# The last quarter of an MLP's second matrix product by seven block products, with its results gathered by adding DMAs

## The chip, the cores and the metric

The kernel runs on one core of one Trainium2 chip. The metric is the device time in microseconds of one execution; three runs of the kernel before took 972.04, 972.15 and 972.39 us, the median is 972.15 us.

## The reference, cut to what matters

The program computes two transformer blocks over 512 tokens of width 1024. The change touches only the very end, the MLP of the second block, and its last line above all:

```python
x = x + gt1 * (mixed @ w_o[l])
h = rmsnorm_2(x, g_norm2[l]) * (1.0 + sc2) + sh2
x = x + gt2 * (jnp.square(jax.nn.relu(h @ w1[l])) @ w2[l])     # w1: 1024 x 4096, w2: 4096 x 1024
```

Everything is float32. The result x is the program's output, 512 x 1024.

## The kernel before, in words

**Exact products from rounded halves.** TensorE reads operands rounded to the type fp32r. Each operand is therefore split in an upper half (`wh`, `ah`, `hh`: a copy to fp32r) and a lower half (`wl`, `al`, `hl`: the value minus the upper half), and a product takes three matmuls (L2109 to L2111, helper `three`): upper by upper, upper by lower, lower by upper. ScalarE (ACT) writes the upper half of each weight (L702), VectorE (DVE) the lower one (L1264), in four pieces of 512 columns per weight unit. A unit is a 128 x 2048 piece of weights, 1 MB, that SP loads into a buffer `raw` (L549). Two buffers each for `wh` and `wl` mean that a unit's halves can be written once the product before the last one is done.

**The MLP in quarters.** The hidden width of 4096 is worked in four quarters of 1024 (`q` = 0 to 3). In a quarter, eight blocks of 128 hidden columns are computed first (`h @ w1`, four weight units, 24 matmuls a block), and ScalarE takes relu and square of each. Then comes the quarter's share of the second product, 512 tokens x 1024 by 1024 x 1024.

**The second product by seven.** In quarters 0 to 2 this share is computed as a 2 x 2 block product in Winograd's form of Strassen's scheme: seven products P1 to P7 of half size (256 tokens, 512 x 512 of weights) where eight are usual, 24 matmuls each (two token blocks `b`, four pieces `k`, three matmuls). It needs sums of blocks of the activations (computed by VectorE in `halves` and split in `s_hi`, `s_lo`) and sums of blocks of the weights. The sums of weights are made while they are loaded: GpSimd (POOL) issues DMAs that add to what SP has put in the buffer (L2088, here "adding loads"). Over the quarters each product is summed up in `sums`, and its combinations give the blocks C11, C12, C21, C22 of the result: C11 = P1 + P2, U2 = P1 + P6, U3 = U2 + P7, C12 = U2 + P5 + P3, C21 = U3 - P4, C22 = U3 + P5.

**The last quarter is computed directly.** For `q` = 3 the share is taken in the usual eight half products: two halves of columns (`ch`) by two halves of the contraction (`kh`), four token blocks, four pieces, three matmuls. Before that, VectorE combines the sums of the first three quarters into the blocks of C (L1899), multiplies them by the gate row `gt` (L1907) and adds them to the residual `x2` (printed as x1b; L1909). As each pair of token block and column half is done on TensorE, VectorE multiplies it by the gate (L1917) and adds it to `x2` (L1920), and ScalarE issues its store to `out` (L1255), eight stores of 256 KB.

**What sets the order.** It is written out by hand: each engine has one instruction stream, and semaphores tie them (`wl` counts lower halves of weights, `w2` and `w1` finished products, `x3` VectorE's work on sums, `acc` ScalarE's copies of products, `w0` to `w3` and `wa0` to `wa3` loads and adding loads by buffer). An engine that waits holds up all that is behind it in its stream.

Of the kernel before, what the change touches and what calls it, by code (L numbers as in the profile page):

```python
# [25 lines left out]
def plan():  # L26
# [103 lines left out]
def program(nc, x, xcols, wall, wf, poolw, params, fng, wada, crow_in, rel, out):  # L130
# [7 lines left out]
    NW = 44 + 3 * 11 + 8  # L138
# [11 lines left out]
    for q_ in range(4):  # L150
        over += [("w1", 8 * q_ + 2 * j + 2) for j in range(4)]
        over += ([("w2", 14 * q_ + 2 * r + 2) for r in range(7)] if q_ < 3 else
                 [("half", 6), ("w2", 46), ("half", 7), ("w2", 50)])
# [9 lines left out]
    with ExitStack() as ctx:  # L163
        def sb(name, shape, dt=F32, where=ctx):
# [126 lines left out]
        s2, junk_2 = (sgt[:, 0:512], sgt[:, 512:1024]), sgt[:, 1024:1536]  # L291
# [4 lines left out]

        sums = {1: (sum_y[:, 0, :], sum_y[:, 1, :]), 7: (sum_y[:, 2, :], sum_y[:, 3, :]),
                6: (sum_y[:, 4, :], sum_y[:, 5, :]), 5: (sum_y[:, 6, :], sum_y[:, 7, :]), 2: (sum_x[:, :], sum_z[:, :])}

        def sems(of, *names):  # L300
# [6 lines left out]
                 "x0", "x1", "x2", "x3", "gf", "g0", "g1", "gt", "x4", "x5", "x6", "x7", "bt0", "bt1", "kd0", "kd1", "vm0", "vm1", "dv0", "dv1", "v2", "out")  # L307

        t = sems("pe_", "half", "ss0", "rb", "zh", "v", "f", "tpc", "za", "qz", "ku", "y", "g", "up", "out", "tp",
# [32 lines left out]
        for w_ in range(NW):  # L342
            q_, r_ = divmod(w_ - W_MLP - 4, 11)
            p_ = PRODUCTS[r_] if 0 <= q_ < 3 and r_ < 7 else 0
# [16 lines left out]
        def hidden_at(n):  # L361

            q, m = divmod(n, 8)
            return s2[n % 2] if q == 3 else s_f[m][:, 0:512] if m < 4 else tmp[:, m % 2, :]
# [2343 lines left out]
```

## Time and profile before

| | us |
|---|---|
| median of three runs | 972.15 |
| profiled execution, its own time | 972.63 |
| its span on the core | 970.8 |
| PE (TensorE matmul) busy | 956.8 (99%) |
| DVE (VectorE) busy | 675.2 (70%) |
| ACT (ScalarE) busy | 547.9 (56%) |
| POOL (GpSimd) busy | 83.6 (9%) |

The profiled execution's own time is 1.8 us above its span; what lies around the span is not in the trace. Times in the trace are microseconds from the span's start. The granted clock of TensorE is 0.999 of full speed over the span, so nothing below turns on it. A matmul's "busy" includes its pipeline: 0.39 us each, although one starts every 0.227 us.

### The profile page before, as it was taken

What the parts mean: (1) busy time and instruction counts of PE and PEld (TensorE: products, weight loads), DVE (VectorE), ACT (ScalarE), POOL (GpSimd) and SP (SyncE); (2) the same over time, 40 slices, a digit from 0 to 9 for tenths busy, and PEclk for the clock granted to TensorE, in tenths of its full rate; (3) what the DMA queues carried; (4) which work ended last, traced back from release to release, by engine and by line L of the source; (5) the groups of instructions that cost most, each with busy time, mean ns of one, the idle gap of its engine ahead of it and who ended that gap; (6) DMA issues with size and microseconds to landing.
All of it is one profiled execution on the core that took longest, in us unless ns stands there. A gap on an engine that the chain in (4) does not pass through costs nothing.

```text
span 970.8 us, 13132 instructions
## 1 busy us (share of the span) xinstructions
PE 956.8 (99%) x4712; PEld 799.6 (82%) x4712; DVE 675.2 (70%) x1237; ACT 547.9 (56%) x1085; POOL 83.6 (9%) x173
## 2 busy tenths in 40 slices
PE   8999999999999999999999999999999999999998
PEld 7878998888888887777788888798888888888886
DVE  6487887878788767667778886756635853774773
ACT  6348776754223357479897664556635544734520
POOL 4001100111121112000000000110000001000000
PEclk9999999999999999999999999999999999999999
DMA  7205222148797644634534224355867568473201
GB/s 297 87 23 188 66 65 100 51 158 349 284 323 282 163 147 154 262 110 121 163 104 129 67 66 172 132 131 130 226 192 193 153 211 191 113 223 124 87 34 54
DMA packets 36674, 148.70 MB, mean 153 GB/s; under 512 B 9193, under 2 KB 9193, under 8 KB 24706
## 3 DMA queue, kind: packets, MB, share of 16 engines
q1 hardware_dynamic: 23970, 101.41, 30.7%
q0 software_dynamic: 9568, 42.48, 16.5%
q10 hardware_dynamic: 3072, 3.98, 1.2%
q8 instruction: 38, 0.62, 0.2%
q14 instruction: 26, 0.21, 0.1%
HBM read 138.32 MB, written 5.27 MB: 148 GB/s over the span
## 4 chain that ended last, share of the span: by engine, by line
PE 86%; DVE 8%; ACT 3%; issue 1%; DMA 1%; POOL 0%; ACTq 0%; DVEq 0%; POOLq 0%
PE psum L2109 25%; PE psum L2111 25%; PE psum L2110 25%; PE psum L2277 3%; PE psum L2256 2%; PE psum L2306 2%; PE psum L2309 1%; DVE wl L1264 1%; DMA raw<-in_wall 1%; ACT two L1009 1%; PE psum L2540 1%; DVE hl L1304 1%; DVE xt L1300 1%; DVE ah L1411 0%; ACT wh L702 0%
## 5 line engine op out<-in xcount | busy, mean ns | idle before, releaser
L2109 PE MATMUL psum<-hh,wh 128*128 128x512 f32 (+1 forms) x720 | 273.6, 380 | 0.7 <-DVE hl L1304 0.6
L2111 PE MATMUL psum<-hh,wl 128*128 128x512 f32 (+1 forms) x720 | 267.4, 371 | 0.0
L2110 PE MATMUL psum<-hl,wh 128*128 128x512 f32 (+1 forms) x720 | 267.2, 371 | 0.0
L1264 DVE TENSOR_TENSOR wl<-raw,wh 128x512 fp32r<-128x512 f32 x328 | 213.9, 684 | 46.2 <-ACT wh L702 45.6
L702 ACT ACTIVATE wh<-raw 128x512 fp32r<-128x512 f32 x328 | 188.6, 620 | 81.3 <-PE psum L2111 64.7
L2109 PEld LDWEIGHTS psum<-hh,wh 128*128 128x128 f32 x720 | 135.3, 188 | 24.2 <-DVE hl L1304 1.4
L2111 PEld LDWEIGHTS psum<-hh,wl 128*128 128x128 f32 x720 | 135.2, 188 | 23.9
L2110 PEld LDWEIGHTS psum<-hl,wh 128*128 128x128 f32 x720 | 135.5, 188 | 21.2 <-issue 1.0
L2109 PE MATMUL psum<-wh,ah 128*128 128x512 f32 x224 | 88.3, 394 | 0.0
L2111 PE MATMUL psum<-wh,al 128*128 128x512 f32 x224 | 87.3, 390 | 0.0
L2110 PE MATMUL psum<-wl,ah 128*128 128x512 f32 x224 | 87.2, 390 | 0.0
L861 ACT ACTIVATE pth<-psum 128x128 fp32r<-128x128 f32 (+4 forms) x104 | 45.9, 442 | 18.0 <-PE psum L2277 17.2
L1181 ACT ACTIVATE two<-psum 128x512 f32<-128x512 f32 x32 | 19.1, 598 | 62.6 <-PE psum L2111 62.6
L2111 PEld LDWEIGHTS psum<-wh,al 128*128 128x128 f32 x224 | 42.1, 188 | 9.0
L2109 PEld LDWEIGHTS psum<-wh,ah 128*128 128x128 f32 x224 | 42.1, 188 | 8.8 <-issue 0.6
L2277 PE MATMUL psum<-ident,p_sb 128*128 128x128 f32 x272 | 46.9, 274 | 2.4 <-DVE ptl L1476 2.3
L1476 DVE TENSOR_TENSOR ptl<-psum,pth 128x128 fp32r<-128x128 f32 (+1 forms) x96 | 46.0, 480 | 4.3 <-ACT pth L861 3.5
L2110 PEld LDWEIGHTS psum<-wl,ah 128*128 128x128 f32 x224 | 42.1, 188 | 7.9
L2277 PEld LDWEIGHTS psum<-ident,p_sb 128*128 128x128 f32 x272 | 33.5, 140 | 13.4 <-issue 5.5
L836 ACT ACTIVATE p_sb<-p_sb,sm 128x528 f32<-128x528 f32 (+3 forms) x64 | 36.1, 564 | 7.7 <-DVE sm L1451 6.8
L842 ACT ACTIVATE p_sb<-p_sb,sm 128x528 f32<-128x528 f32 (+3 forms) x64 | 35.6, 559 | 0.3
L2109 PE MATMUL psum<-wh,hh 128*128 128x512 f32 x76 | 30.9, 407 | 1.5 <-DVE wl L1264 0.9
(336 smaller groups left out, 1631.1 us busy)
## 6 DMA issues: line engine op xcount, KB each, us to landing
raw<-in_wall SPq DMA_DIRECT2D x78, 1024.0 KB, 5.3
raw<-in_wall POOLq DMA_DIRECT2D x15, 1024.0 KB, 7.8
wa<-in_wada POOLq DMA_DIRECT2D x24, 512.0 KB, 5.9
gt<-in_wada POOLq DMA_DIRECT2D x20, 512.0 KB, 6.2
xt<-in_xcols SPq DMA_DIRECT2D x8, 264.0 KB, 8.4
cb<-c_rows SPq DMA_DIRECT2D x8, 264.0 KB, 3.1
x<-in_x SPq DMA_DIRECT2D x4, 512.0 KB, 10.2
x_kept<-x SPq DMA_DIRECT2D x4, 512.0 KB, 2.8
```

The costliest lines, as they stand in the source:

```text
L702: e.activation(home(w)[0][:, 512 * c:512 * c + 512], raw_of(w, c), ACT.Copy).then_inc(a["wh"], 1)
L836: e.activation(block_p(h, i), block_p(h, i), ACT.Exp, bias=nmx, scale=1.0 if h in FG else -1.0, accum_out=su).then_inc(a["exp"], 1)
L842: e.activation(block_p(h, i), block_p(h, i), ACT.Copy, scale=mx).then_inc(a["norm"], 1)
L861: e.activation(ph[0:rows, PT[j]:PT[j] + w_], bank[bk][0:rows, 0:w_], ACT.Copy).then_inc(a["turn"], 1)
L1264: e.tensor_tensor(home(w)[1][:, cs], raw_of(w, c), home(w)[0][:, cs].bitcast(F32), ALU.subtract).then_inc(v["wl"], 1)
L1476: e.tensor_tensor(dst, bank[bk][0:rows, 0:w_], ph[0:rows, o:o + w_].bitcast(F32), ALU.subtract).then_inc(v["turn"], 1)
L2109: e.matmul(out_, lh, rh, start=start, stop=False, skip_group_check=True)
L2110: e.matmul(out_, lh, rl, start=False, stop=False, skip_group_check=True)
L2111: return e.matmul(out_, ll, rh, start=False, stop=stop, skip_group_check=True)
L2256: ins = e.matmul(dst[:, size * j:size * j + size], q[:, 128 * i:128 * i + 128], k[:, size * j:size * j + size], start=k is k_up, stop=k is ...
L2277: ins = e.transpose(bank[bk][:, 128 * (i - i0):128 * (i - i0) + 128], head(h)[0][:, o:o + 128], ident[:, :])
L2306: ins = e.matmul(out_bank(h)[:, 128 * i0:512], lhs, ph[:, PT[j]:PT[j] + w_], start=(j == 3 and h not in SB), stop=j < 0, skip_group_check= ...
```

## The change

The last quarter's share of the second product is computed by seven products as well, in an order of its own (`LAST_ORDER`: P1, P2, P6, P5, P7, P4, P3). P1, P6, P7 and P4 of it follow one another in the same two PSUM banks, so that U2, U3 and the last quarter's C21 arise there by accumulation; ScalarE copies P1, U2 and U3 out on the way (`last_copy`). P3 is accumulated on P5.

The blocks of C of the first three quarters are still combined by VectorE and multiplied by the gate, but no longer added to the residual by VectorE: GpSimd issues adding DMAs from one place of SBUF to another, two of 256 KB for each of six blocks (`to_residual`: c12, c21, c11, c22, and of the last quarter 11 and 22). They share one semaphore, `res`, and each pair waits for the pair before it to land. The adding load for P4's weights (T4) stands ahead of the last five of these pairs in GpSimd's stream. C21 and C12 of the last quarter are added by VectorE (`last_21`, `last_12`).

SP issues four of the eight stores, for C11 after five pairs (`res` 160) and for C22 after all six (`res` 192); ScalarE issues the other four. SP loads one weight unit more, GpSimd five adding loads more.

```diff
-        for ch, kh in ((0, 0), (1, 1), (1, 0), (0, 1)) if q < 3 else ((0, 0), (0, 1), (1, 0), (1, 1)):
+        for ch, kh in ((0, 0), (1, 1), (1, 0), (0, 1)):
...
-PRODUCTS = (1, 2, 7, 6, 5, 3, 4)
+ORDER = (1, 2, 7, 6, 5, 3, 4)
+LAST_ORDER = (1, 2, 6, 5, 7, 4, 3)
 P_BANK = {1: (2, 3), 2: (0, 1), 7: (2, 3), 6: (0, 1), 5: (2, 3), 3: (4, 5), 4: (6, 7)}
+LAST_BANK = {1: (4, 5), 2: (2, 3), 6: (4, 5), 5: (6, 7), 7: (4, 5), 4: (4, 5), 3: (6, 7)}
 GATHERED = (1, 2, 7, 6, 5)
+def order(q):
+    return ORDER if q < 3 else LAST_ORDER
 X3 = [(q, p, b) for q in (1, 2) for p in GATHERED for b in range(2)]
-X3 += [(3, name, b) for name in ("u2", "u3", "c12a", "c22", "c11", "c12", "c21") for b in range(2)]
-X3 += [(3, op, ch, i) for ch in range(2) for i in range(4) for op in ("*c", "+c")]
-X3 += [(3, op, ch, i) for ch in range(2) for i in range(4) for op in ("*", "+")]
+X3 += [(3, name, b) for name in ("u2", "u3", "c12a", "c12", "c22", "c21", "c11", "*c12", "*c21", "*c11", "*c22",
+                                 "p11", "*11", "*u", "-u", "p22", "*22", "*21", "+21") for b in range(2)]
+X3 += [(3, op, b) for b in range(2) for op in ("*12", "+12")]
...
             o_ = W_MLP + 11 * q_ + 4
-            place.update(zip(range(o_, o_ + 11), (a2, a3, a0, a1, a2, a3, a1, a0, a2, a3, a1) if q_ < 3 else places[q_]))
+            place.update(zip(range(o_, o_ + 11), (a2, a3, a0, a1, a2, a3, a1, a0, a2, a3, a1) if q_ < 3 else
+                             (a2, a3, a0, a2, a1, a0, a3)))
...
+        block_at = {"c11": sums[1], "c12": sums[6], "c21": sums[7], "c22": sums[5]}
+        p1_last = sums[2]
+        u2_last, u3_last = (s_f[0][:, 0:512], s_f[1][:, 0:512]), (s_f[2][:, 0:512], s_f[3][:, 0:512])
...
-                load(u + 4 + (1 if q < 3 else 0), a0)
+                load(u + 4 + 1, a0)
                 e.wait_ge(v["wl"], 4 * (o + 1) + 4)
                 load(u + 4 + 1, a1)
                 e.wait_ge(v["wl"], 4 * (o + 2) + 4)
-                load(u + 4 + (0 if q < 3 else 2), a2)
+                load(u + 4, a2)
                 e.wait_ge(v["wl"], 4 * (o + 3) + 4)
                 load(u + 4 + 3, a3)
+                e.wait_ge(v["wl"], 4 * (o + 5) + 4)
+                load(u + 4 + 1, a3)
                 if q < 3:
-                    e.wait_ge(v["wl"], 4 * (o + 5) + 4)
-                    load(u + 4 + 1, a3)
...
+            for ch, i0, count in ((0, 0, 160), (1, 2, 192)):
+                e.wait_ge(d["res"], count)
+                for i in (i0, i0 + 1):
+                    e.dma_start(out[128 * i:128 * i + 128, 512 * ch:512 * ch + 512],
+                                x2[:, i, 512 * ch:512 * ch + 512]).then_inc(d["out"], 16)
...
+            def last_copy(r, b):
+                e.wait_ge(t["w2"], 42 + 2 * r + b + 1)
+                if r == 0:
+                    e.wait_ge(v["x3"], N_X3[3, "c11", b])
+                else:
+                    e.wait_ge(v["sl"], 48)
+                e.activation({0: p1_last, 2: u2_last, 4: u3_last}[r][b], bank[4 + b], ACT.Copy).then_inc(a["acc"], 1)
...
+                    if q == 3 and r % 2:
+                        for b in range(2):
+                            last_copy(r - 1, b)
...
+            for b in range(2):
+                e.wait_ge(v["x3"], N_X3[3, "+21", b])
+                store(2 + b, 0)
+            for b in range(2):
+                e.wait_ge(v["x3"], N_X3[3, "+12", b])
+                store(b, 1)
...
+            def gated(name, b):
+                c, ch = block_at[name][b], int(name[2]) - 1
+                if (name, b) == ("c12", 0):
                     e.wait_ge(d["gt"], 32)
-                e.wait_ge(v["x3"], N_X3[3, {(0, 0): "c11", (0, 1): "c12", (1, 0): "c21", (1, 1): "c22"}[i // 2, ch], b])
+                e.wait_ge(v["x3"], N_X3[3, name, b])
                 e.tensor_tensor(c, c, gt[:, 1, 512 * ch:512 * ch + 512], ALU.mult).then_inc(v["x3"], 1)
...
+            def last_21(op, b):
+                c, o = tmp[:, b, :], x2[:, 2 + b, 0:512]
+                if op == "*21":
+                    e.wait_ge(t["w2"], 42 + 10 + b + 1)
+                    e.tensor_tensor(c, bank[4 + b], gt[:, 1, 0:512], ALU.mult).then_inc(v["x3"], 1)
+                else:
+                    e.wait_ge(v["x3"], N_X3[3, "*21", b])
+                    e.wait_ge(d["res"], 64)
+                    e.tensor_tensor(o, o, c, ALU.add).then_inc(v["x3"], 1)
+            def last_12(b):
+                c, o = u2_last[b], x2[:, b, 512:1024]
+                e.wait_ge(t["w2"], 42 + 12 + b + 1)
+                e.wait_ge(v["x3"], N_X3[3, "-u", b])
+                e.tensor_tensor(c, bank[6 + b], gt[:, 1, 512:1024], ALU.mult).then_inc(v["x3"], 1)
...
+                    if q == 3 and r == 0:
+                        last_step(gated, "c21")
+                    elif q == 3 and r == 1:
+                        last_step(gated, "c11", "c22")
+                    elif q == 3 and r == 2:
+                        last_step(last_11, "p11")
+                    elif q == 3 and r == 3:
+                        last_step(last_11, "*11")
+                    elif q == 3 and r == 4:
+                        last_step(last_u, "*u", "-u")
+                    elif q == 3 and r == 5:
+                        last_step(last_22, "*22")
+            last_step(last_21, "*21", "+21")
+            for b in range(2):
+                last_12(b)
...
+            def to_residual(name):
+                n = TO_RESIDUAL.index(name)
+                if n:
+                    e.wait_ge(d["res"], 32 * n)
+                src = {"*11": p1_last, "*22": u3_last}[name] if n > 3 else block_at[name[1:]]
+                for b in range(2):
+                    i, ch = 2 * (int(name[-2]) - 1) + b, int(name[-1]) - 1
+                    e.wait_ge(v["x3"], N_X3[3, name, b])
+                    e.dma_start(x2[:, i, 512 * ch:512 * ch + 512], src[b], accum_op=ALU.add).then_inc(d["res"], 16)
...
+                if q < 3:
+                    e.wait_ge(d[f"w{place[o3]}"], 16 * n_load[o3])
+                    add(q, 2, place[o3])
+                e.wait_ge(d[f"w{place[o2]}"], 16 * n_load[o2])
+                add(q, 2, place[o2])
+                e.wait_ge(d[f"wa{place[o2]}"], 192 + 16 * n_add[o2] - 16)
+                add(q, 0, place[o2])
+                if q == 3:
+                    e.wait_ge(d[f"w{place[o3]}"], 16 * n_load[o3])
+                    add(q, 2, place[o3])
+                    to_residual("*c12")
                 e.wait_ge(v["wl"], 4 * o + 4)
                 add(q, 2, a2)
-                e.wait_ge(v["wl"], 4 * (o + 3) + 4)
-                add(q, 3, a1)
+                e.wait_ge(v["wl"], 4 * o2 + 4)
+                add(q, 3, place[o2])
                 if q == 0:
                     gate(1)
+            to_residual("*c21")
+            to_residual("*c11")
+            to_residual("*c22")
+            to_residual("*11")
+            to_residual("*22")
...
+            def last_product(r):
+                p, w = LAST_ORDER[r], W_MLP + 37 + r
+                upper, lower = home(w)
+                for b in range(2):
+                    if p == 1:
+                        e.wait_ge(v["x3"], N_X3[3, "c12", b])
+                    elif p == 2:
+                        e.wait_ge(a["r"], 30)
+                    elif p == 5:
+                        e.wait_ge(v["x3"], N_X3[3, "c21", b])
+                    elif p == 3:
+                        e.wait_ge(v["x3"], N_X3[3, "p22", b])
+                    else:
+                        e.wait_ge(a["acc"], 10 + {6: 0, 7: 2, 4: 4}[p] + b + 1)
+                    for k in range(4):
+                        if b == 0:
+                            e.wait_ge(v["wl"], 4 * w + k + 1)
+                            e.wait_ge(v["sl"], n_sl(3, k if p in (1, 7) else 4 + k, p in (5, 6, 3)))
+                        o = slice(512 * k, 512 * k + 512)
+                        ins = three(bank[LAST_BANK[p][b]], *factor(p, k, b), upper[:, o], lower[:, o],
+                                    k == 0 and p in (1, 2, 5), k == 3)
                     ins.then_inc(t["w2"], 1)
...
-            for m in range(4):
-                w, ch, kh = W_MLP + 37 + m, m // 2, m % 2
-                for i in range(4):
-                    if m == 0:
-                        e.wait_ge(v["x3"], N_X3[3, "c12" if i < 2 else "c21", i % 2])
-                    for k in range(4):
-                        if i == 0:
-                            e.wait_ge(v["wl"], 4 * w + k + 1)
-                            if ch == 0:
-                                e.wait_ge(v["sl"], 36 + 4 * kh + k + 1)
-                        ins = by_rows(w, k, 4 * kh + k, bank[i + (0 if ch else 4)], (ah, al), 128 * i, 128,
-                                      kh == 0 and k == 0, kh == 1 and k == 3)
-                    if kh:
-                        ins.then_inc(t["w2"], 1)
-                if kh == 0:
-                    ins.then_inc(t["half"], 1)
...
+                    product(q, r) if q < 3 else last_product(r)
```

The helpers `last_11`, `last_u` and `last_22` follow the same pattern as `last_21`: `p11` adds P2 from PSUM to the copy of P1, `*11` multiplies by the gate, `*u` and `-u` multiply U2's copy and subtract it from `x2`, `p22` takes U3's copy and P5 from PSUM together, `*22` multiplies by the gate; each is one VectorE instruction for each of two token blocks.

GpSimd's stream from the third quarter's last adding loads on. Before, it ends there:

```order
L2088 DMA raw3<-in_wall 128x2048 [waits dma_w3]
L2088 DMA raw<-in_wall 128x2048 [waits dma_w2]
L2088 DMA raw<-in_wall 128x2048 [waits dma_wa2]
L2088 DMA raw<-in_wall 128x2048 [waits dve_wl] x2
L163 UNCONDITIONAL_BRANCH
```

In the changed kernel, from the fourth quarter's weights on (`raw` and `raw3` are weight buffers, x1b is the residual, the sources are gated blocks of C):

```order
L2172 DMA raw3<-in_wall 128x2048 [waits dma_wa3]
L2172 DMA raw<-in_wall 128x2048 [waits dma_w0]
L2185 DMA x1b<-sum_y 128x512 [waits dve_x3] x2
L2172 DMA raw<-in_wall 128x2048 [waits dve_wl]
L2172 DMA raw3<-in_wall 128x2048 [waits dve_wl]
L2185 DMA x1b<-sum_y 128x512 [waits dve_x3,dma_res]
L2185 DMA x1b<-sum_y 128x512 [waits dve_x3]
L2185 DMA x1b<-sum_y 128x512 [waits dve_x3,dma_res]
```

Five adding loads and twelve adding DMAs into the residual are new; the last ten of the twelve stand behind the adding load for P4, which waits for VectorE's lower half of P6's weights.

VectorE's stream over its last rows before, the fourth column half of the direct product:

```order
L1264 TENSOR_TENSOR wl<-raw,wh 128x512 x4
L1917 TENSOR_TENSOR tmp<-psum,gt 128x512
L1920 TENSOR_TENSOR x1b<-x1b,tmp 128x512
L1917 TENSOR_TENSOR tmp<-psum,gt 128x512
L1920 TENSOR_TENSOR x1b<-x1b,tmp 128x512
```

And in the changed kernel, from P7's weights on (wl is P7's, then P4's, then P3's lower half; sum_x, sum_z the copy of P1, sgt that of U2, gt and s_y that of U3):

```order
L1296 TENSOR_TENSOR wl<-raw,wh 128x512 x4
L1953 TENSOR_TENSOR sum_x<-sum_x,gt 128x512
L1953 TENSOR_TENSOR sum_z<-sum_z,gt 128x512
L1296 TENSOR_TENSOR wl<-raw,wh 128x512 x4
L1960 TENSOR_TENSOR sgt<-sgt,gt 128x512 x2
L1964 TENSOR_TENSOR x1b<-x1b,sgt 128x512 x2
L1971 TENSOR_TENSOR gt<-psum,gt 128x512
L1971 TENSOR_TENSOR s_y<-psum,s_y 128x512
L1296 TENSOR_TENSOR wl<-raw,wh 128x512 x4
L1974 TENSOR_TENSOR gt<-gt 128x512
L1974 TENSOR_TENSOR s_y<-s_y,gt 128x512
```

The work on results now stands between the lower halves of the weights in every product, and the last block that goes by DMA (L1974, `*22`) is ready only after P3's weights. The last two pairs of instructions on VectorE (L1991, L1993) are of the same kind as before. SP's stream ends, in the changed kernel, with the stores:

```order
L565 DMA raw<-in_wall 128x2048 [waits dve_wl] x31
L707 DMA out<-x1b 128x512 [waits dma_res]
L707 DMA out<-x1b 128x512
L707 DMA out<-x1b 128x512 [waits dma_res]
L707 DMA out<-x1b 128x512
L172 UNCONDITIONAL_BRANCH
```

Before, nothing follows the loads on SP.

## Rows read from the trace of the kernel before

**Rows 1.** Page: busy time by engine, and the chain that ended last.

```profile
PE 956.8 (99%) x4712; PEld 799.6 (82%) x4712; DVE 675.2 (70%) x1237; ACT 547.9 (56%) x1085; POOL 83.6 (9%) x173
...
PE 86%; DVE 8%; ACT 3%; issue 1%; DMA 1%; POOL 0%; ACTq 0%; DVEq 0%; POOLq 0%
```

**Rows 2.** Stretches: us, busy (x) PE, PEld, DVE, ACT, POOL; PEclk, DMA share, GB/s.

```profile
920.00:940.00 20.00, 20.00 (x90) 16.57 (x89) 14.72 (x24) 6.10 (x11) 0.00 (x0) 1.00 0.04 14
940.00:960.00 20.00, 20.00 (x90) 16.57 (x89) 8.78 (x14) 2.83 (x5) 0.00 (x0) 1.00 0.11 40
960.00:971.00 11.00, 6.84 (x31) 5.32 (x29) 4.28 (x7) 0.00 (x0) 0.00 (x0) 0.92 0.25 95
```

**Rows 3.** Timeline of VectorE, the end: start, busy, line, tiles, [idle <-releaser].

```profile
958.72 0.69 DVE L1917 TENSOR_TENSOR tmp<-psum,gt 128x512 f32<-128x512 f32 x1 [8.55 <-PE psum L2111]
...
964.16 0.69 DVE L1917 TENSOR_TENSOR tmp<-psum,gt 128x512 f32<-128x512 f32 x1 [1.30 <-PE psum L2111]
...
966.88 0.69 DVE L1917 TENSOR_TENSOR tmp<-psum,gt 128x512 f32<-128x512 f32 x1 [1.30 <-PE psum L2111]
967.60 0.69 DVE L1920 TENSOR_TENSOR x1b<-x1b,tmp 128x512 f32<-128x512 f32 x1
```

**Rows 4.** One line's instructions: ScalarE's stores (L1255).

```profile
L1255 ACTq DMA_DIRECT2D out<-x1b x8: 338/339/357, 938.4 to 968.3; - x8
...
DMA to landing us min/median/max: 2.0/2.1/2.6
```

**Rows 5.** Timeline of ScalarE: the last relu of the third and fourth quarter.

```profile
841.66 0.60 ACT L1181 ACTIVATE two<-psum 128x512 f32<-128x512 f32 x1 [1.41 <-PE psum L2111]
...
845.08 4.26 ACT L702 ACTIVATE wh<-raw 128x512 fp32r<-128x512 f32 x8
...
923.36 0.60 ACT L1181 ACTIVATE two<-psum 128x512 f32<-128x512 f32 x1 [2.99 <-PE psum L2111]
```

**Rows 6.** Timeline of VectorE in the third quarter's products.

```profile
842.95 0.43 DVE L1858 TENSOR_TENSOR s_y<-tmp,s_y 128x256 f32<-128x256 f32 x1 [1.02 <-ACT tmp L1197]
...
846.09 2.49 DVE L1264 TENSOR_TENSOR wl<-raw,wh 128x512 fp32r<-128x512 f32 x4
...
853.30 2.50 DVE L1264 TENSOR_TENSOR wl<-raw,wh 128x512 fp32r<-128x512 f32 x4
```

**Rows 7.** Timeline of GpSimd: its adding loads in the third quarter.

```profile
800.85 0.88 POOL L2088 DMA_DIRECT2D raw<-in_wall  x1 [25.52 <-DMA raw<-in_wall]
812.99 0.87 POOL L2088 DMA_DIRECT2D raw<-in_wall  x1 [11.27 <-DMA raw<-in_wall]
821.12 0.86 POOL L2088 DMA_DIRECT2D raw<-in_wall  x1 [7.25 <-DMA raw<-in_wall]
842.29 0.86 POOL L2088 DMA_DIRECT2D raw<-in_wall  x1 [20.31 <-DVE wl L1264]
856.17 0.88 POOL L2088 DMA_DIRECT2D raw<-in_wall  x1 [13.03 <-DVE wl L1264]
```

**Rows 8.** GpSimd's adding loads (L2088), from 780 us on: issue to landing.

```profile
L2088 POOL DMA_DIRECT2D raw<-in_wall x5: 859/869/877, 800.9 to 856.2; - x5
...
DMA to landing us min/median/max: 7.7/7.9/8.0
```

**Rows 9.** DMA by queue, 842 to 851 us, one adding load: packets, MB, share.

```profile
q0 software_dynamic: 144, 1.05, 61.6%
```

**Rows 10.** DMA by queue, 958 to 971 us, the last four stores.

```profile
q10 hardware_dynamic: 576, 1.05, 21.4%
```

**Rows 11.** GpSimd's plain load of 512 KB (L2041) issued at 400.5 us.

```profile
L2041 POOL DMA_DIRECT2D wa<-in_wada x1: 528/528/528, 400.5 to 400.5; - x1
...
DMA to landing us min/median/max: 3.7/3.7/3.7
```

**Rows 12.** Timeline of VectorE: combining eight blocks of sums in the fourth quarter.

```profile
893.29 4.89 DVE L1899 TENSOR_TENSOR sum_y<-sum_y 128x512 f32<-128x512 f32 x8
```

More of the change, by code:

```diff
@@ L151, in program @@
         over += [("w1", 8 * q_ + 2 * j + 2) for j in range(4)]
-        over += ([("w2", 14 * q_ + 2 * r + 2) for r in range(7)] if q_ < 3 else
-                 [("half", 6), ("w2", 46), ("half", 7), ("w2", 50)])
+        over += [("w2", 14 * q_ + 2 * r + 2) for r in range(7)]
     assert len(over) == NW
@@ L343, in program @@
             q_, r_ = divmod(w_ - W_MLP - 4, 11)
-            p_ = PRODUCTS[r_] if 0 <= q_ < 3 and r_ < 7 else 0
+            p_ = order(q_)[r_] if q_ >= 0 and r_ < 7 else 0
             loaded_[place[w_]] += p_ not in (4, 5)
@@ L1192, in square @@
                 dst, src = hidden_at(n), two[:, n % 2, :]
[L1193 removed]
+                if m < 4:
                     dst = s_f[m].rearrange("p (a b) -> p a b", a=3)[:, 0::2, :]
@@ L1200, in hidden_upper @@
                 q, m = divmod(n, 8)
-                if q < 3 and (m < 4 or part):
+                if m < 4 or part:
                     e.wait_ge(v["s"], 16 * q + (m + 1 if m < 4 else 3 * m - 5))
@@ L1873, in hidden @@
             def hidden(n):
-                if n < 24:
-                    halves(n)
+                halves(n)
                 hidden_lower(n)
-                if n < 24 and n % 8 > 3:
+                if n % 8 > 3:
                     hidden_lower(n, 1)
             def gather(q, p, b):
-                e.wait_ge(t["w2"], 14 * q + 2 * PRODUCTS.index(p) + b + 1)
+                e.wait_ge(t["w2"], 14 * q + 2 * ORDER.index(p) + b + 1)
                 if q == 1:
@@ L1922, in _, with last_step @@
+            def last_step(f, *ops):
+                for op in ops:
+                    for b in range(2):
+                        f(op, b)
             for q in range(4):
@@ L1933, in _ @@
                     if q == 3 and j < 2:
-                        for name in (("u2", "u3", "c12a", "c22"), ("c11", "c12", "c21"))[j]:
-                            for b in range(2):
-                                blocks(name, b)
+                        last_step(blocks, *(("u2", "u3", "c12a", "c12"), ("c22", "c21", "c11"))[j])
                     elif q == 3 and j == 2:
-                        for i in range(4):
-                            add_block(0, i)
-                if q == 3:
-                    break
-                for r, p in enumerate(PRODUCTS):
+                        last_step(gated, "c12")
+                for r in range(7):
                     w = W_MLP + 11 * q + 4 + r
-                    if q and r and PRODUCTS[r - 1] in sums:
+                    if q in (1, 2) and r and ORDER[r - 1] in sums:
                         for b in range(2):
-                            gather(q, PRODUCTS[r - 1], b)
-                    for c in range(4):
-                        lower(w + 1, c)
-            for m in range(4):
-                for s_ in range(8):
-                    slot(W_MLP + 37 + m, s_)
-                    if m % 2 and s_ % 2:
-                        add_last(m // 2, s_ // 2)
-                    if m == 0 and s_ % 2:
-                        add_block(1, s_ // 2)
+                            gather(q, ORDER[r - 1], b)
+                    if q == 3 and r == 5:
+                        last_step(last_22, "p22")
+                    if w + 1 < NW:
+                        for c in range(4):
+                            lower(w + 1, c)
+                    if q == 3 and r == 0:
[13 more added lines that the diff above has]
+                last_12(b)
         @block.gpsimd
```

125 lines of the change are left out of this document (64 added, 61 removed).

## The prediction

> **What bounds the kernel now.** I read the page first: TensorE is busy 99% of the span and makes 86% of the chain that ended last [rows 1]. Then the stretches of the last 50 us: 20.00 us of 20 busy twice, at full granted clock, and in the last eleven 6.84 us, while the DMA engines carry 4 to 25% [rows 2]. So TensorE's stream of matmuls sets the end, and behind its last one a short tail. Its pace comes from VectorE's last rows: a new block of twelve matmuls is taken over every 2.72 us (964.16, 966.88) [rows 3], so a matmul costs 2.72/12 = 0.2267 us. The tail: the last block is multiplied at 966.88, added at 967.60 (to 968.29), its store issued, and the span ends at 970.8 [rows 3]: 3.9 us after the last matmul, 2.5 us of it after the addition; a store lands 2.0 to 2.6 us after issue [rows 4].
>
> **Matmuls.** The direct share is 2 column halves x 2 halves of the contraction x 4 token blocks x 4 pieces x 3 = 192 matmuls, the share by products 7 x 24 = 168. 24 fewer at 0.2267 us are 5.44 us. If nothing else became late, TensorE would end at 961.4 instead of 966.9, the last addition at 962.85, and the span at 965.4.
>
> **Can the weights and sums keep up?** The third quarter is the model, since it does the same by seven. A quarter is (8 + 7) x 24 matmuls = 81.6 us, and the last relu of the two quarters begins at 841.66 and 923.36, 81.7 apart [rows 5]. There ScalarE writes P2's upper halves from 845.08 and VectorE its lower halves from 846.09 [rows 5, 6]; P2 starts at 841.5 + 5.44 = 846.9, and TensorE was not held. Carried over by 81.6: products start at 923.2 (P1), 928.6 (P2), 934.1 (P6), 939.5 (P5), 945.0 (P7), 950.4 (P4) and 955.8 (P3). Ahead of them VectorE has the extra work of `halves` again (pieces of 0.43 us [rows 6]) and the same 14 combinations as now, at 0.61 us each (eight in 4.89 [rows 12]), while of the eight gate multiplications and additions in this stage two multiplications stay. Laid out row by row at these lengths, each weight piece is ready about 1 us or more ahead of its use, except P2's first, with about 0.4 us, as in the third quarter. In the products' stage VectorE has 16 us for six further weight units (2.50 each [rows 6], 15 us) and 26 instructions on results at 0.6 to 0.7 us, 17 us: 32 of 38 us. It is kept busy but in each product the weights come first or after at most four such instructions. P6's unit is the one I need below: ScalarE ends P2's at 928.9, copies P1 out twice (0.6 each), VectorE does the two multiplications of c21 to 931.3, then P6's lower half from 931.3 to 933.8, before P6 starts at 934.1 for its first piece by 2 us. P4's end leaves VectorE with `p22`, 1.3 us, and P3's weights, done by 954.4, ahead of 955.8. Cost 0, with 1 us as my upper bound.
>
> **Adding loads.** Five more of 1 MB. They land 7.7 to 8.0 us after issue [rows 8]. P5's is released by P1's lower half, at about 923.7 (842.29 in the third quarter, and 81.6 on) and lands by 931.9; ScalarE can use it from 934.1. P4's is issued about 0.4 us after P6's lower half (853.30 + 2.50, issued at 856.17 [rows 6, 7]), so at 934.2, and lands at 941.9; it is wanted at 945.0. Both cost 0, with 2 to 3 us of cover.
>
> **The chain of adding DMAs.** This is where I expect the end to be set. Behind P4's adding load in the same stream and queue come five pairs of 256 KB, and each pair waits for the landing of the one before. What a link costs, from rows: an adding load keeps its queue busy 61.6% of 9 us on 16 engines, so 5.54 us each for 1 MB [rows 9], or 1.39 us for 256 KB at the same rate, about twice the plain rate (four stores: 21.4% of 13 us, 0.70 us each [rows 10]), as it has two sources to read. Issue and completion are the rest, 7.7 - 5.54 = 2.16 us. GpSimd needs 0.43 us from a landing to the next issue (821.12 - 812.99 - 7.7 [rows 7]). For a pair: 2.16 + 2 x 1.39 + 0.43 = 5.37 us. I take 5.1, since the issue of a smaller DMA is shorter (0.53 for 512 KB against 0.86 [rows 8, 11]). Bounds: 2.9 us (a plain 256 KB store lands in 2.1 [rows 4], a second 0.34 later, and the wake-up 0.43), and 13.6 us, if each packet of 2 KB took as long as one of 8 KB (2.16 + 2 x 5.54 + 0.43).
>
> Sum: c21's pair waits in the queue behind P4's load, 941.9 + 2 x 1.39 = 944.7. Then c11, c22, 11 and 22, four links of 5.1: 965.1. The last pair's data is ready at 955.6 (behind P3's weights) and does not matter. c12's pair is early, issued about 919. SP wakes (0.3), issues C22's two stores 0.34 apart, the last at 965.7, and 2.4 us later the span ends: 968.1, where TensorE's own path ends at 965.4. Of 5.44 us, 2.7 are given back.
>
> The Trainium skill, "DMA: Bandwidth & Descriptors", section "Anatomy of one DMA — SWDGE (gpsimd) path", gives for a DMA from GpSimd about 2.0 us plus bytes over 436e3 per us. For 1 MB that is an estimate of 4.4 us; the trace disagrees for DMAs that add, with 7.7 [rows 8], while its fixed part agrees with the 2.16 left over above. By that rule a pair would cost about 3.6 us with the wake-up, and the chain would be covered: this is the first rival's time.
>
> Against the medians: the profiled execution took 972.63 us, 1.8 above its span, and the median is 0.5 lower. I take 2.7 from the median: 969.4.
>
> **Rivals.**
> - *The chain is covered* (25%). The end by the chain is 944.7 + 4 x link + 3.0; it equals TensorE's 965.4 at a link of 4.4 us. For it: source and target both lie in SBUF, the nearest row (7.7) has an HBM source; and the fixed part may be less for a small DMA. Against: twice 1.39 us of transfer are already 2.8. Time: 972.15 - 5.4 = 966.7.
> - *The chain costs more than the products save* (12%): slower than before. It decides at a link above 5.8 us (944.7 + 4 x 5.8 + 3.0 = 970.9), and would be measured as slower from 6.3. The mechanism: an adding packet of 2 KB is dearer per byte than one of 8 KB, because reading both operands, adding and writing has a cost of its own for each packet. For it: nothing in the trace has ever added rows under 8 KB. Against: plain packets of 2 KB move at the rate of larger ones, 256 KB in 0.70 us. At half the 8 KB packet's time for each 2 KB packet, a pair costs 2.16 + 5.54 + 0.43 = 8.1, c21 lands at 947.4, and the median would be 972.15 + (947.4 + 32.4 + 3.0 - 970.8) = 984.2. At 6.5 it would be 975.
> - *TensorE is held* (8%): P5's load or VectorE's heavier stream is late. For it: P2's first piece has only 0.4 us. Against: the third quarter shows the same margin without a stall, and every other wait has 1 us or more. A stall of up to 2.7 us hides behind the chain, except one ahead of P6's weights, which moves P4's load and the whole chain with it: with 1.5 us there, 970.9.
> - *The change does not save matmuls' time* (3%), as accumulating four products in one pair of banks made each wait for ScalarE's copies. P4 follows P7 directly: its first block needs the copy of P7's first, 2.7 us after that was done, and a copy takes 0.6. Covered; if not, up to 3 us, and 969 to 970.
>
> **How the numbers follow.** Forecast, the chain set the end with a link between 4.4 and 5.8 us: 52%, 969.4, its own range 967 to 971.9. About 0.2% (1.9 us) is what a measurement of this kernel can tell from no change, so faster means under 970.2, a link under 5.3. I give two thirds of the forecast case to that side: 0.35; with 0.25 for the covered chain and about 0.05 of the small cases it is 0.65. Same: the rest of the forecast (0.17) and parts of the others (0.06), 0.23. Slower 0.12. The range reaches from the covered chain, 966.5, to a link of 5.9 us, 972.5; outside lie most of the slower rival and a little below.
>
> **What would show it.** In the profile after: 168 matmuls behind the last relu at one per 0.227 us, and VectorE's last multiplication at 961.4 instead of 966.88; GpSimd's rows of L2185 from 934.9 on in pairs, 5.1 us from pair to pair, the last at about 960.5; SP's last store (L707) 3 us after ScalarE's last (L1259, 962.9), and the chain of waits that ended last going through SP and GpSimd's DMAs, no longer through VectorE and TensorE. I am wrong if the pairs follow in under 4.4 us or over 5.8, if P4's adding load is not issued near 934.2, or if TensorE shows idle time among the last seven products.

## The result, and the profile after

| | before | after |
|---|---|---|
| median, us | 972.27 (4 runs) | 977.29 (4 runs, 976.98 to 977.68) |
| ratio to before | 1 | 1.0053, 95% interval 1.0041 to 1.0065 |
| profiled execution: span, us | 970.8 | 975.5 |

The kernel became 5.0 us slower, 0.5%, where 2.7 us faster were forecast. The page of the changed kernel, busy time by engine and the chain that ended last which answer to [rows 1]:

```profile
PE 950.7 (97%) x4688; PEld 795.4 (82%) x4688; DVE 688.7 (71%) x1265; ACT 560.6 (57%) x1107; POOL 98.3 (10%) x190
...
PE 79%; DVE 9%; issue 4%; ACT 4%; DMA 3%; POOL 1%; POOLq 0%; ACTq 0%; DVEq 0%
```

TensorE is busy 6.1 us less, 5.4 of them for 24 matmuls fewer (the other 0.7 I did not follow), but its share of the span has fallen from 99% to 97%, and "issue" and DMA, 1% of the chain each before, now make 4% and 3% of it. Where TensorE stopped is read from the stretches (columns as in [rows 2]):

```profile
955.00:960.00 5.00, 5.00 (x24) 4.15 (x23) 3.77 (x6) 0.00 (x0) 0.86 (x1) 1.00 0.70 176
960.00:965.00 5.00, 0.82 (x4) 0.36 (x2) 1.38 (x2) 0.00 (x0) 1.02 (x2) 1.00 0.70 176
965.00:970.00 5.00, 0.00 (x0) 0.00 (x0) 0.00 (x0) 0.00 (x0) 1.57 (x2) 0.51 0.58 157
```

TensorE is busy without a gap to 960 and for 0.82 us more. From 965 to the end of the span at 975.5, for 10.5 us, no compute engine does anything but GpSimd, which issues two DMAs. (The granted clock of 0.51 in the last row is that of a TensorE that has nothing left to do; it costs nothing here.) VectorE's last two rows answer to [rows 3]:

```profile
960.86 0.69 DVE L1991 TENSOR_TENSOR sgt<-psum,gt 128x512 f32<-128x512 f32 x1 [1.30 <-PE psum L2219]
961.58 0.69 DVE L1993 TENSOR_TENSOR x1b<-x1b,sgt 128x512 f32<-128x512 f32 x1
```

The last multiplication begins at 960.86, where 961.4 was forecast; 0.7 us of that is the start: ScalarE's last relu begins at 922.66 where it was 923.36 [rows 5], and GpSimd's first load near 200 us is as much earlier, long before anything that was changed. From relu to last multiplication it is 38.2 us, and before it was 43.5: 5.3 us saved by the products, as worked out.

So the products did their part and the chain of adding DMAs took it back, and 5 us more. GpSimd's timeline from P4's adding load on (L2172; start, length, line, tiles, [idle before it <-releaser]):

```profile
933.63 0.89 POOL L2172 DMA_DIRECT2D raw<-in_wall  x1 [9.38 <-DVE wl L1296]
934.25 2.06 POOL L2185 DMA_DIRECT2D x1b<-sum_y  x2
944.40 0.86 POOL L2185 DMA_DIRECT2D x1b<-sum_y  x1 [8.09 <-DMA x1b<-sum_y]
948.04 0.88 POOL L2185 DMA_DIRECT2D x1b<-sum_y  x1 [2.79 <-issue]
951.67 1.75 POOL L2185 DMA_DIRECT2D x1b<-sum_y  x2 [2.75 <-DMA x1b<-sum_y]
956.94 0.86 POOL L2185 DMA_DIRECT2D x1b<-sum_x  x1 [3.52 <-DMA x1b<-sum_y]
961.23 0.87 POOL L2185 DMA_DIRECT2D x1b<-sum_z  x1 [3.43 <-issue]
964.85 0.87 POOL L2185 DMA_DIRECT2D x1b<-gt  x1 [2.75 <-DMA x1b<-sum_z]
968.99 0.86 POOL L2185 DMA_DIRECT2D x1b<-s_y  x1 [3.27 <-issue]
```

P4's load is issued at 933.63 (forecast 934.2), c21's pair right behind it; the pair has landed at 944.06 (forecast 944.7), and c11's first DMA is issued at 944.40. Up to here every step came within 0.7 us, as much as the whole stage is early. Then the second DMA of c11 starts at 948.04 and not at 945.3. The idle 2.79 us before it is put to "issue": no semaphore explains it. The same before the second DMAs of block 11 (961.23) and of block 22 (968.99), while c22's two follow each other at once (951.67, x2). The chain that ended last shows it from the other side (start, length, what):

```profile
944.40 0.86 POOL x1b L2185
945.26 2.77 issue
...
948.04 3.33 DMA x1b<-sum_y
```

Each DMA so held is issued about 0.3 us after the one before it has landed: 944.40, landed 3.3 us later, then 948.04. One DMA of 256 KB that runs alone lands 3.3 us after its issue (line L2185, the minimum); the longest, 9.3, is c21's behind P4's load:

```profile
DMA to landing us min/median/max: 3.3/4.0/9.3
```

SP's stores follow the chain (four, the last issued at 972.7, 2.8 us ahead of the span's end):

```profile
L707 SPq DMA_DIRECT2D out<-x1b x4: 333/388/433, 964.6 to 972.7; - x4
```

### The profile page after: what moved, and what is told of

Its sections match the earlier page's. It is cut to its first block, busy times and chain, and to the rows that moved or that the text cites. A ratio compares the mean times of both kernels' runs of the same rounds, so it can differ in the third digit from the quotient of the medians.

```text
span 975.5 us, 13190 instructions
## 1 busy us (share of the span) xinstructions
PE 950.7 (97%) x4688; PEld 795.4 (82%) x4688; DVE 688.7 (71%) x1265; ACT 560.6 (57%) x1107; POOL 98.3 (10%) x190
## 4 chain that ended last, share of the span: by engine, by line
PE 79%; DVE 9%; issue 4%; ACT 4%; DMA 3%; POOL 1%; POOLq 0%; ACTq 0%; DVEq 0%
PE psum L2217 23%; PE psum L2219 22%; PE psum L2218 22%; PE psum L2385 3%; PE psum L2364 2%; DVE wl L1296 2%; DMA x1b<-sum_y 2%; PE psum L2414 2%; PE psum L2417 1%; DMA raw<-in_wall 1%; ACT two L1030 1%; PE psum L2648 1%; DVE hl L1336 1%; DVE xt L1332 1%; DVE tmp L1809 0%
## 5 line engine op out<-in xcount | busy, mean ns | idle before, releaser
L1296 DVE TENSOR_TENSOR wl<-raw,wh 128x512 fp32r<-128x512 f32 x340 | 221.2, 685 | 45.4 <-ACT wh L723 44.8
L723 ACT ACTIVATE wh<-raw 128x512 fp32r<-128x512 f32 x340 | 194.9, 620 | 69.8 <-PE psum L2219 64.7
L2217 PE MATMUL psum<-wh,ah 128*128 128x512 f32 x192 | 76.1, 396 | 0.0
L2219 PE MATMUL psum<-wh,al 128*128 128x512 f32 x192 | 75.0, 390 | 0.0
L2218 PE MATMUL psum<-wl,ah 128*128 128x512 f32 x192 | 74.9, 390 | 0.0
L2172 POOL DMA_DIRECT2D raw<-in_wall x20 | 17.4, 868 | 261.0 <-DMA raw<-in_wall 145.6
L2217 PEld LDWEIGHTS psum<-wh,ah 128*128 128x128 f32 x192 | 36.1, 188 | 7.8 <-issue 0.8
L2219 PEld LDWEIGHTS psum<-wh,al 128*128 128x128 f32 x192 | 36.1, 188 | 7.6
L857 ACT ACTIVATE p_sb<-p_sb,sm 128x528 f32<-128x528 f32 (+3 forms) x64 | 36.1, 564 | 7.6 <-DVE sm L1483 6.8
L2219 PE MATMUL psum<-wh,s_y 128*128 128x512 f32 x96 | 37.4, 389 | 0.0
## 6 DMA issues: line engine op xcount, KB each, us to landing
x<-in_x SPq DMA_DIRECT2D x4, 512.0 KB, 10.2
```

Of the source, the lines that this page charges most:

```text
L723: e.activation(home(w)[0][:, 512 * c:512 * c + 512], raw_of(w, c), ACT.Copy).then_inc(a["wh"], 1)
L857: e.activation(block_p(h, i), block_p(h, i), ACT.Exp, bias=nmx, scale=1.0 if h in FG else -1.0, accum_out=su).then_inc(a["exp"], 1)
L1296: e.tensor_tensor(home(w)[1][:, cs], raw_of(w, c), home(w)[0][:, cs].bitcast(F32), ALU.subtract).then_inc(v["wl"], 1)
L2217: e.matmul(out_, lh, rh, start=start, stop=False, skip_group_check=True)
L2218: e.matmul(out_, lh, rl, start=False, stop=False, skip_group_check=True)
L2219: return e.matmul(out_, ll, rh, start=False, stop=stop, skip_group_check=True)
```

## The experiments

Each run below was measured beside the kernel before, which gave 971.8 to 971.9 us then and 972.27 beside the changed kernel. So up to 0.5 us of a difference to the changed kernel may be the round's and not the edit's. Where a time is of one run, it is worth about 1 us: the ten runs with the larger ring lie between 971.48 and 972.82.

**A larger ring.**

```diff
-    nc = bacc.Bacc("TRN2", ..., dynamic_dma_scratch_size=1024)
+    nc = bacc.Bacc("TRN2", ..., dynamic_dma_scratch_size=1280)
```

 Theory 2 (an adding DMA waits for the one before it into the same residual tensor, whatever the ring): three waits inside pairs of the same length and 977.3 within 0.7. Theory 3 (VectorE's reads of SBUF hold GpSimd's issue up): likewise no change.

Measured: 971.88 us, ratio to before 1.000 (0.9991 to 1.001), 5.4 us faster than the changed kernel. GpSimd's timeline:

```profile
944.26 1.76 POOL L2185 DMA_DIRECT2D x1b<-sum_y  x2 [8.21 <-DMA x1b<-sum_y]
950.03 1.75 POOL L2185 DMA_DIRECT2D x1b<-sum_y  x2 [4.01 <-DMA x1b<-sum_y]
955.15 0.86 POOL L2185 DMA_DIRECT2D x1b<-sum_x  x1 [3.37 <-DMA x1b<-sum_y]
955.69 1.20 POOL L2185 DMA_DIRECT2D x1b<-sum_z  x1
961.23 0.87 POOL L2185 DMA_DIRECT2D x1b<-gt  x1 [4.34 <-DMA x1b<-sum_z]
961.77 1.22 POOL L2185 DMA_DIRECT2D x1b<-s_y  x1
```

No wait within a pair is left: c11's and c22's two are one row (x2, 1.75 us), and those of 11 and 22 stand 0.54 us apart. The last pair has landed at 967.2. Only the bytes reserved for GpSimd's DMAs were changed; with the same tensors added to and the same work on VectorE, theories 2 and 3 would have kept the waits. Theory 1 stands, as far as that a larger reserve takes them away. The links are now 5.77, 5.12 and 6.08 us from pair to pair.

The same edit shortened a wait far from the end, between two DMAs of 2 KB each that have no semaphore between them and nothing to do with the residual. With 1024 bytes the second started 11.03 us after the first (317.62 and 328.65); now it is 2.89 (317.17 and 320.06), and it no longer waits for the first to land, which takes 8.2 us:

```profile
317.17 0.80 POOL L2096 DMA_DIRECT2D gate_rows<-mod  x1
320.06 0.77 POOL L2096 DMA_DIRECT2D gate_rows<-mod  x1 [2.09 <-issue]
```

**A smaller ring.**

```diff
-    ... dynamic_dma_scratch_size=1024)
+    ... dynamic_dma_scratch_size=768)
```

> The ring gets 768 bytes instead of 1024. Theory 1: the second DMA of more pairs waits, c22's among them, which was issued at once before; up to 3 us longer, 977.3 to 981. Theories 2 and 3: no change, the same three pairs split.

Measured: 974.21 us in one run, faster than with 1024, so the expectation on the time was wrong. But waits put to "issue" came at new places: one of 10.20 us in front of an adding load of weights, and one of 6.88 us in front of c21's second DMA:

```profile
901.09 0.88 POOL L2172 DMA_DIRECT2D raw<-in_wall  x1 [10.20 <-issue]
...
933.83 1.14 POOL L2185 DMA_DIRECT2D x1b<-sum_y  x1
941.86 0.87 POOL L2185 DMA_DIRECT2D x1b<-sum_y  x1 [6.88 <-issue]
...
954.51 0.86 POOL L2185 DMA_DIRECT2D x1b<-sum_y  x1 [2.65 <-DVE gt L1974]
958.20 0.87 POOL L2185 DMA_DIRECT2D x1b<-sum_x  x1 [2.84 <-DMA x1b<-sum_y]
958.74 1.23 POOL L2185 DMA_DIRECT2D x1b<-sum_z  x1
```

So c21's second was held until about the landing of P4's load (941.5). In front of c22's second (954.51) GpSimd stood idle for 2.65 us too; the trace names an instruction of VectorE as releaser, but this is only inferred: in the changed kernel that DMA went out at 952.20, before that instruction (953.69 there). Blocks 11 (958.20, 958.74) and 22 were not split. Theories 2 and 3 expected the same three waits, and theory 1 more of them than with 1024 bytes; neither came. Which DMA waits is thus not a matter of size alone: of the last four links only one has a wait inside its pair here.

**One more DMA, long before.** This asks whether the place in the ring decides.

```diff
-                if q == 0:
+                if q in (0, 1):
                     gate(1)
...
-                    e.wait_ge(d["gt"], 32)
+                    e.wait_ge(d["gt"], 48)
```

> The changed kernel with one more GpSimd DMA of 512 KB early in the MLP (the gate row is loaded a second time in the second quarter, 180 us ahead of the end), ring 1024 as in the changed kernel. If the place in the ring decides which DMA waits (theory 1), the waits inside the last pairs fall on other DMAs: c11's second, block 11's second and block 22's second waited 2.8 to 3.4 us before, now at least one of the three does not and another may; the time moves by up to 3 us either way. If the waits belong to these DMAs themselves, they are the same three and the time is 977.3.

Measured: 977.69 us in one run, with waits in front of the same three DMAs (the first is put to VectorE here, with the same 2.79 us that stood at "issue" before; its data can't be late, since the run with 1280 bytes issued that DMA at once):

```profile
948.74 0.86 POOL L2185 DMA_DIRECT2D x1b<-sum_y  x1 [2.79 <-DVE sgt L1960]
...
961.67 0.87 POOL L2185 DMA_DIRECT2D x1b<-sum_z  x1 [3.16 <-issue]
...
969.45 0.86 POOL L2185 DMA_DIRECT2D x1b<-s_y  x1 [3.29 <-issue]
```

An additional DMA at 774.8, 174 us ahead of the first that is held, moved nothing. That part of theory 1, a count of DMAs over the whole program that decides which one is held, is not borne out; what does decide stays open.

**One DMA for a block.**

```diff
+                if n < 4:
+                    e.wait_ge(v["x3"], N_X3[3, name, 1])
+                    e.dma_start(x2[:, i:i + 2, 512 * ch:512 * ch + 512], sum_y[:, k:k + 2, :],
+                                accum_op=ALU.add).then_inc(d["res"], 32)
+                    return
```

> Each of the blocks c12, c21, c11 and c22 goes by one adding DMA of 512 KB instead of two of 256 KB; blocks 11 and 22 by two as before; ring and semaphores as in the changed kernel. Theory 1 (a DMA waits for room only while an earlier one is under way): none of the 512 KB DMAs waits, since each is issued after the landing of the one before. A link is 2.1 us fixed + 16 packets of 0.187 us for each engine + 0.4 = 5.5 us, so c22 lands at about 955, 1 to 2 us earlier than in the changed kernel, and the median is 975 to 976.5. If a wait belonged to every second DMA into the residual, whatever its size, a 3 us wait would show between these too, and the time would stay at 977.

Measured: 973.72 us in one run, 3.6 us faster than the changed kernel and 1.3 less than the least expected.

```profile
944.71 1.22 POOL L2185 DMA_DIRECT2D x1b<-sum_y  x1 [8.81 <-DMA x1b<-sum_y]
950.15 1.20 POOL L2185 DMA_DIRECT2D x1b<-sum_y  x1 [4.21 <-DMA x1b<-sum_y]
955.53 0.91 POOL L2191 DMA_DIRECT2D x1b<-sum_x  x1 [4.19 <-DMA x1b<-sum_y]
959.27 0.88 POOL L2191 DMA_DIRECT2D x1b<-sum_z  x1 [2.83 <-DVE sgt L1991]
963.48 0.87 POOL L2191 DMA_DIRECT2D x1b<-gt  x1 [3.33 <-DMA x1b<-sum_z]
964.01 1.21 POOL L2191 DMA_DIRECT2D x1b<-s_y  x1
```

The links of 512 KB are 5.44 and 5.38 us, where 5.5 were expected, without a wait. Of the two pairs that stayed, block 11's was split (959.27, 2.83 us idle) and 22's was not; the expectation had left both as they were.

**Semaphores of their own.** c21, c11 and c22 are no longer ordered by waits; 11 and 22 wait only for the blocks to whose place they add.

```diff
-                if n:
-                    e.wait_ge(d["res"], 32 * n)
+                for x, count in {"*11": (("res", 32), ("g0", 64)), "*22": (("crow", 48), ("gt", 64))}.get(name, ()):
+                    e.wait_ge(d[x], count)
...
-                    e.dma_start(..., accum_op=ALU.add).then_inc(d["res"], 16)
+                    e.dma_start(..., accum_op=ALU.add).then_inc(d[OWN[n]], 16)
```

> The blocks no longer share one semaphore: c21, c11 and c22 are issued without waiting for each other, only blocks 11 and 22 wait for c11 and c22, to whose places in the residual they add. Theory 1 (the ring): three or more of the DMAs of c21, c11 and c22 still wait about 3 us each for room, but the first halves no longer wait for a landing; the chain up to c22 ends 3 to 6 us earlier, the last store is then set by block 22 (ready at 955): 969 to 974. Theory 2 (each adding DMA waits for the one before): six DMAs at 3.6 us, c22 lands at 962, no better than 2 us: 975 to 977. If neither holds and only the semaphore costs time: six DMAs one behind another at 1.5 us, c22 lands by 953, and the end is block 22's pair, issued at 955.1, landed by 960: 967.

Measured: 967.69 us, ratio 0.9956 (0.9942 to 0.9971).

```profile
933.73 0.89 POOL L2172 DMA_DIRECT2D raw<-in_wall  x1 [9.38 <-DVE wl L1296]
934.28 2.13 POOL L2186 DMA_DIRECT2D x1b<-sum_y  x2
942.01 0.86 POOL L2186 DMA_DIRECT2D x1b<-sum_y  x1 [5.60 <-issue]
...
952.50 0.87 POOL L2186 DMA_DIRECT2D x1b<-sum_z  x1 [1.92 <-issue]
...
956.15 0.86 POOL L2186 DMA_DIRECT2D x1b<-s_y  x1 [0.23 <-issue]
```

Waits for room are still there: 942.01 is held 5.60 us, until P4's load (issued at 933.73) has landed, at 941.7. But a wait of 2 or 3 us now costs only itself. Block 22 goes out at 955.06 and 956.15, and the end is TensorE's. The time is below the 969 to 974 expected for the ring, and near the 967 expected if only the shared semaphore cost time: the waits for room came, but off the path that sets the end.

**c21 ahead of P4's adding load.** This undoes that part of the change.

```diff
                 add(q, 2, a2)
+                if q == 3:
+                    to_residual("*c21")
                 e.wait_ge(v["wl"], 4 * o2 + 4)
...
-            to_residual("*c21")
```

> c21's pair stands ahead of P4's adding load in GpSimd's stream, all else as in the changed kernel. If the chain of pairs sets the end, link by link: c21 is issued at 931 instead of 934 and lands at about 936 instead of 944; c11 is issued at 936.5 behind P4's load (issued 933.6, landed 941.5) and lands at 945 instead of 951: the chain ends one link, 6 to 8 us, earlier, the span at 968 to 970 and the median at 970 to 972. P4's weights stay early enough. If the end is TensorE's, no change.

Measured: 971.14 us, ratio 0.9991 (0.9982 to 1.0001), 6.2 us faster than the changed kernel: one link, as expected. TensorE was not held by P4's weights.

**Blocks 11 and 22 by VectorE.**

```diff
+            def add_11_22(name, b):
+                ...
+                e.tensor_tensor(o, o, c, ALU.add).then_inc(v["x3"], 1)
             last_step(last_21, "*21", "+21")
-            for b in range(2):
-                last_12(b)
+            last_step(add_11_22, "+11")
+            last_12(0)
+            last_step(add_11_22, "+22")
+            last_12(1)
...
-            to_residual("*11")
-            to_residual("*22")
```

> Blocks 11 and 22 of the last quarter are added to the residual by VectorE (four additions at 0.6 us in its last rows), so the chain of adding DMAs has only c12, c21, c11 and c22 and ends where c22 lands, 956.5 in the profile after. If the chain of DMAs is what set the end: the last addition on VectorE ends at about 962.4 instead of 962.3, the end is TensorE's again, and the median is 966.5 to 967.5. If the end had another cause (TensorE or the stores), it stays at 975 to 978.

Measured: 967.29 us, ratio 0.9954 (0.9937 to 0.997). The last addition on VectorE, where 961.58 stood after the change:

```profile
961.18 0.68 DVE L1991 TENSOR_TENSOR sgt<-psum,gt 128x512 f32<-128x512 f32 x1
961.90 0.69 DVE L1993 TENSOR_TENSOR x1b<-x1b,sgt 128x512 f32<-128x512 f32 x1
```

Two links fewer, and 10.0 us gone: the chain of DMAs was the end's cause. c11's second DMA was split here too (948.37), and nothing came of it.

**All six by VectorE,** without any adding DMA into the residual; the additions stand right behind their multiplications or up to two products later (`+c12`, `+c21`, `+c11`, `+c22`), and those of 11 and 22 as above.

> No adding DMA into the residual at all: VectorE adds all six blocks (twelve additions, 7.3 us, eight of them before or among the products). VectorE had about 4.3 us idle in the stage of the products, so it is full there. If its slack carries this: lower halves of weights come up to 1.2 us later, ahead of their use by about 0.5 us, and the median is 967 to 968, which would say that GpSimd's DMAs were not needed. If not: TensorE waits at P5 or P3, 1 to 3 us, 968 to 970.5.

Measured: 968.22 us, ratio 0.9961 (0.9947 to 0.9975). The stretches:

```profile
950.00:955.00 5.00, 5.00 (x24) 4.14 (x23) 5.00 (x9) 2.68 (x5) 0.00 (x0) 1.00 0.00 0
...
960.00:965.00 5.00, 1.68 (x8) 1.06 (x6) 4.32 (x7) 0.00 (x0) 0.00 (x0) 0.93 0.91 338
```

TensorE has no gap among the products, but VectorE is full and behind at the very end: its last multiplication begins at 962.98, 1.8 us after that of the run before this one. The time lies in the range expected for a TensorE that is held, but what is late is VectorE's own last rows.

**The best version:** own semaphores, block 11 by DMAs, block 22 by VectorE.

```diff
             last_step(last_21, "*21", "+21")
-            for b in range(2):
-                last_12(b)
+            last_12(0)
+            last_step(add_22, "+22")
+            last_12(1)
...
-            to_residual("*22")
```

> Semaphores of their own for the blocks, as in the run with own semaphores, block 11 by adding DMAs, block 22 by VectorE: two additions fewer in VectorE's last rows than with both, and no DMA chain near the end. VectorE is then idle ahead of TensorE's last block, as it was before the change. The end is TensorE's alone: 0.2 to 0.4 us under the run in which VectorE adds both, 966.9 to 967.2.

Measured: 966.72 us, ratio 0.9945 (0.993 to 0.996), 5.2 us faster than before, 10.6 faster than the changed kernel, and a little below the expected 966.9 to 967.2. Its span of 965.0 is within 0.4 of the 965.4 worked out for TensorE's own path. The same with the ring of 1280 bytes:

> The best version so far (own semaphores, block 22 by VectorE) with the ring of 1280 bytes. Its span ended with TensorE's last block and the short tail, with no DMA chain at the end, so more room in the ring should give nothing: 966.7 within 0.4. If a wait for room still held something on the path, it would fall to about 966.

Measured: 966.80 us, ratio 0.9949 (0.9932 to 0.9966): no difference, as expected. But its timeline shows that 1280 bytes do not end the waits:

```profile
933.59 0.88 POOL L2179 DMA_DIRECT2D raw<-in_wall  x1 [9.33 <-DVE wl L1296]
934.13 2.99 POOL L2193 DMA_DIRECT2D x1b<-sum_y  x3
942.06 0.88 POOL L2193 DMA_DIRECT2D x1b<-sum_y  x1 [4.93 <-issue]
```

Behind P4's load, three further DMAs go out here and the fourth is held until that load has landed, at 941.8. With 1024 bytes it was two, and the third was held (own semaphores, 942.01); with 768 it was one, and the second was held (941.86). So with the load itself two, three and four DMAs were under way: one more for every 256 bytes. This is what theory 1 asks for, and not what a mere shift of tensors in memory by the same edit, which no run separates, would be expected to give. It does not explain the waits inside the last pairs, where only one earlier DMA was still under way.

## Why the prediction was wrong

- **Matmuls, 5.44 us: right.** 43.5 against 38.2 us from the last relu to the last multiplication, and the best version gives back 5.2 us of it.
- **Weights, sums and adding loads in time: right.** TensorE shows no idle time among the last products, and P4's load was issued at 933.6 (934.2 forecast) and c21 landed at 944.1 (944.7).
- **That the chain of pairs sets the end: right**, and shown by three edits that shorten it in different ways and leave the products alone (c21 ahead, 11 and 22 by VectorE, own semaphores): 6.2, 10.0 and 9.6 us less. The last two end on TensorE's path, so they do not price a link.
- **The cost of a link, 5.1 us: wrong; this is the step that failed.** Four links, from c21's landing at 944.1 to the last landing at 972.3 (968.99 + 3.3), took 28.2 us, 7.1 each, where 20.4 were forecast. With the larger ring the same four links took 23.3 us (943.9 to 967.2), so 4.9 us of the difference of 7.8 are the waits that the larger ring takes away (the medians differ by 5.4). The forecast took it that the second DMA of a pair is issued as soon as GpSimd has issued the first; three of four were held until the first had landed. Why these three is open. The remaining 2.9 us are the link itself, 5.8 us on average without a wait. The 5.37 us that the rows gave were nearer than the 5.1 that I chose; the deduction for a shorter issue was a mistake: the issue of an adding DMA of 256 KB takes 0.86 us as that of 1 MB.
- **The price of a packet was nearly right.** Block 22's second DMA kept its queue busy for 42.3% of the 3.6 us from 968.9 to 972.5, 1.52 us on each engine, where 1.39 were taken from the 1 MB loads [rows 9]. So the slower rival's packets of 2 KB are dearer per byte by about a tenth, and not by half or double (they also come from SBUF and not from HBM, which no run separates). Its outcome came, and its threshold, a link of 5.8 us, held on both sides: at 7.1 the change lost, and at 5.8, with the larger ring, the kernel was level with before. A mechanism that was not on my list carried the link past it.
- **The first rival's rule** (2.0 us plus bytes over 436e3 in the Trainium skill, "DMA: Bandwidth & Descriptors", section "Anatomy of one DMA — SWDGE (gpsimd) path") gives 2.6 us for one of these 256 KB; the trace has 3.3, so it is short for adding DMAs of this size too.
- **A row of before could have warned me.** There GpSimd issues two DMAs of 2 KB each in a row, with no semaphore between them, and its timeline puts 10 us between:

```profile
318.65 0.80 POOL L2012 DMA_DIRECT2D gate_rows<-mod  x1
329.52 0.77 POOL L2012 DMA_DIRECT2D gate_rows<-mod  x1 [10.06 <-issue]
```

The same "issue" stands there; I had read it over, since it was far from the end. In the changed kernel it recurs (10.23 us), and with the larger ring it falls to 2.09.

## What to carry to other kernels

A run of DMAs from GpSimd that are chained by one semaphore is priced by the landing of each, not by its transfer: four links of 256 KB pairs cost 28 us where moving their data takes 12 (eight times 1.5). Here it paid to give independent transfers semaphores of their own (9.6 us) and to put short additions near the end on an engine that had slack there (10.0 us). Look in the timeline for "issue" idle time between two DMAs of GpSimd before adding more of them. An error in the price of one link counts once for every link: here 0.7 us was 2.9.

## What the runs showed of the hardware

- GpSimd's issue of a DMA can be held until earlier DMAs of its own queue have landed, and this depends on the bytes reserved for its DMAs. Counting a 1 MB adding load at their head, two DMAs were under way at 768 bytes, three at 1024 and four at 1280 before the next was held, for 6.9, 5.6 and 4.9 us. Of the last pairs, chained by a semaphore, none was split at 1280 bytes, three at 1024 and two at 768, where a wait of 10.2 us came at another place. Which DMA of those is held was not settled: one more DMA long before did not shift it; with one DMA for a block, or semaphores of their own, others were held.
- An adding load of 1 MB in 8 KB packets from HBM kept each engine busy for 5.54 us [rows 9], one of 256 KB in 2 KB packets from SBUF to SBUF for 1.52 us; a plain store's 256 KB took 0.70 us [rows 10]. The adding one of 256 KB lands 3.3 us after its issue when it is alone; the two that were issued beside stores to `out` (956.94 and 964.85) took 4.1 and 3.9.
